# Down matrices of 32 experts: two 2 MB transfers into two ring slots, or one 4 MB transfer into both

## The reference

```python
h = jax.nn.silu(jnp.einsum('td,edf->tef', t, w1)) * jnp.einsum('td,edf->tef', t, w3)
h = h * gate[:, :, None].astype(h.dtype)
y = jnp.einsum('tef,efd->td', h, w2)
```

## Time and profile before

| | us |
|---|---|
| median of 3 runs | 1423.67 (1422.31 to 1424.02) |
| the profiled execution | 1424.06 |
| its span | 1422.3 |
| PE busy | 1359.1 (96%) |
| the chain that ended last, by engine | PE 63%, DMA 18%, DVE 2% |
| DVE, ACT, POOL busy | 539.5, 345.4, 229.4 |
| moved by DMA | 471.66 MB, 332 GB/s over the span |
| the expert transfers | 192 of 2 MB |

### The profile page before, as it was taken

One profiled execution on the slowest core, in us unless ns is written; L12 is line 12 of the kernel. 1 busy time (PEld: TensorE's weight loads), 2 busy tenths in 40 slices (PEclk: granted clock), 3 DMA queues, 4 the chain that ended last, 5 costly groups with the idle time before them and its releaser, 6 DMA issues.

```text
span 1422.3 us, 19177 instructions
## 1 busy us (share of the span) xinstructions
PE 1359.1 (96%) x7242; PEld 766.9 (54%) x7242; DVE 539.5 (38%) x1027; ACT 345.4 (24%) x618; POOL 229.4 (16%) x205
## 2 busy tenths in 40 slices
PE   8999999999999999998998999999999999899896
PEld 7884898987786345434433533544544543443353
DVE  6999420544425233233313323223323231331325
ACT  1121378566571111110210110111111020111102
POOL 2002656687881000000000000000000000000000
PEclk9999999999998999999999999999999999999999
DMA  8533543444475999999999999959999999999992
GB/s 213 178 119 118 207 178 119 156 141 166 139 287 237 388 428 427 429 428 427 429 428 429 429 429 429 428 217 430 429 428 429 428 429 428 429 429 429 428 428 121
DMA packets 71389, 471.66 MB, mean 332 GB/s; under 512 B 17313, under 2 KB 17394, under 8 KB 46130
## 3 DMA queue, kind: packets, MB, share of 16 engines
q1 hardware_dynamic: 70690, 469.75, 80.6%
q10 hardware_dynamic: 528, 1.05, 0.2%
q0 software_dynamic: 128, 0.26, 0.1%
HBM read 468.95 MB, written 2.10 MB: 331 GB/s over the span
## 4 chain that ended last, share of the span: by engine, by line
PE 63%; DMA 18%; DVE 2%; ACT 1%; POOL 1%; issue 1%; DVEq 0%; POOLq 0%; ACTq 0%
PE ps L1870 25%; DMA ring<-in_expert_w_dram 18%; PE ps L1888 12%; PE ps L1528 11%; PE ps L1848 5%; PE ps L1878 3%; PE ps L1899 2%; PE ps L1900 2%; POOL w_lo L558 1%; PE ps L1860 1%; PE ps L1820 1%; PE ps L1795 0%; DVE reg_y L1110 0%; PE ps L1702 0%; DVE reg_x L1463 0%
## 5 line engine op out<-in xcount | busy, mean ns | idle before, releaser
L1888 PE MATMUL ps<-ring,reg_y 128*64 128x512 f32 x1056 | 238.8, 605 | 9.7 <-DVE reg_y L1377 7.8
L558 POOL TENSOR_TENSOR w_lo<-ring,w_hi 128x512 fp32r<-128x512 f32 x152 | 200.0, 1349 | 72.3 <-ACT w_hi L620 71.1
L1383 DVE TENSOR_TENSOR y_lo_t<-ps,y_hi_t 64x512 fp32r<-64x512 f32 x132 | 90.9, 689 | 214.9 <-ACT y_hi_t L852 213.6
L852 ACT ACTIVATE y_hi_t<-ps 64x512 fp32r<-64x512 f32 x132 | 78.1, 592 | 317.9 <-PE ps L1888 315.5
L1888 PEld LDWEIGHTS ps<-ring,reg_y 128*64 128x64 f32 x1056 | 75.4, 139 | 146.7 <-issue 141.5
L1392 DVE TENSOR_TENSOR reg_x<-ps,reg_x 128x512 f32<-128x512 f32 x136 | 87.2, 683 | 137.3 <-PE ps L1900 137.3
L1870 PE MATMUL ps<-reg_e,reg_s 128*64 128x512 f32 x528 | 119.5, 594 | 11.7 <-POOLq L583 11.7
L1870 PE MATMUL ps<-ring,reg_s 128*64 128x512 f32 x528 | 120.0, 596 | 6.8 <-POOLq L583 6.2
L1870 PE MATMUL ps<-ring,reg_y 128*64 128x512 f32 x528 | 120.0, 596 | 6.8 <-POOLq L583 6.2
L1870 PE MATMUL ps<-reg_e,reg_y 128*64 128x512 f32 x528 | 119.5, 594 | 3.2 <-POOLq L583 3.0
L1372 DVE TENSOR_SCALAR reg_y<-ps,lamv 128x512 f32<-128x512 f32 x33 | 24.8, 750 | 244.8 <-PE ps L1870 244.8
(11 more groups left out here) (397 smaller groups left out, 1759.2 us busy)
## 6 DMA issues: line engine op xcount, KB each, us to landing
ring<-in_expert_w_dram SPq DMA_DIRECT2D x128, 2048.0 KB, 20.7
reg_e<-in_expert_w_dram SPq DMA_DIRECT2D x64, 2048.0 KB, 20.9
ring<-in_w_in_dram SPq DMA_DIRECT2D x19, 2048.0 KB, 8.1
ring<-in_w_out_dram SPq DMA_DIRECT2D x8, 2048.0 KB, 8.0
reg_x<-in_x_dram SPq DMA_DIRECT2D x4, 1024.0 KB, 8.5
ring<-in_w_in_dram SPq DMA_DIRECT2D x2, 1024.0 KB, 6.7
out_dram<-reg_x SPq DMA_DIRECT2D x4, 512.0 KB, 2.7
reg_e<-in_ssm_w_glu_dram ACTq DMA_DIRECT2D x1, 1024.0 KB, 9.1
```

Of the source, the lines that this page charges most:

```text
L558: G.tensor_tensor(w_lo[:, i % BUFS, :], unit(u % SLOTS_A)[:, c, :], w_hi[:, i % BUFS, :], ALU.subtract).then_inc(row_lo, 1)
L852: A.activation(y_hi_t[64 * q:64 * q + 64, 512 * k:512 * k + 512], psb[3 + k // 2][64 * (k % 2):64 * (k % 2) + 64, :], cp).then_inc(e_yhi, 1)
L1383: last = V.tensor_tensor(y_lo_t[64 * q:64 * q + 64, w], psb[3 + k // 2][64 * (k % 2):64 * (k % 2) + 64, :], y_hi_t[64 * q:64 * q + 64, w], ...
L1888: last = M(psb[3 + i // 2][64 * (i % 2):64 * (i % 2) + 64, :], hT[:, 2 * half + f, :], unit2(s)[:, f, 512 * i:512 * i + 512], start=half = ...
```

## The change

The down matrix of an expert is now viewed with 4 rows of 8 KB a partition, which are 32 KB in one piece in HBM, and goes in one transfer of 4 MB into ring slots 2 and 3 taken as one tile. Before, each half was a transfer of 16 KB a partition into one slot. SP waits for `slot_free` at the count of piece 5 (both slots free) before it issues this transfer. Its completion raises only the semaphore of ring slot 2, and POOL then raises `e_in` by 2. PE's program is unchanged: `unit2` of slots 2 and 3 finds the same data, since piece 4 was and is the first 16 KB of each partition's 32 KB. The transfers of `w1` and `w3` are unchanged.

```diff
-        w2_v = e_w2.rearrange("l e (p h c) n -> p (l e) h c n", h=2, p=P)
+        w2_v = e_w2.rearrange("l e (p c) n -> p (l e) c n", p=P)
+        w2_slots = ring4[:, 2 * UW:4 * UW].rearrange("p (c n) -> p c n", n=D)
...
             def item(n_, e):
 
-                for k in range(6):
+                for k in range(4):
                     s = slot_of(k)
                     sp.wait_ge(slot_free, n_ * 6 + k + 1)
-                    w = (w1_v, w3_v, w2_v)[k // 2]
-                    src = w[:, ds(e, 1), k % 2, :, :]
-                    sp.dma_start(unit(s) if k < 4 else unit2(s), src.rearrange("p e c n -> p (e c) n")).then_inc(ring_in[s], 16)
+                    src = (w1_v, w3_v)[k // 2][:, ds(e, 1), k % 2, :, :]
+                    sp.dma_start(unit(s), src.rearrange("p e c n -> p (e c) n")).then_inc(ring_in[s], 16)
+                sp.wait_ge(slot_free, n_ * 6 + 6)
+                sp.dma_start(w2_slots, w2_v[:, ds(e, 1), :, :].rearrange("p e c n -> p (e c) n")).then_inc(ring_in[slot_of(4)], 16)
...
             def item_landed(e):
 
-                for k in range(6):
+                for k in range(5):
                     s = slot_of(k)
                     base = 16 * (UNITS_A // SLOTS_A) if s < SLOTS_A else 0
                     g.wait_ge(ring_in[s], e * 16 + base + 16)
-                    g.sem_inc(e_in, 1)
+                    g.sem_inc(e_in, 2 if k == 4 else 1)
```

## The result

The changed kernel takes 1428.89 us in the median of 6 runs (1428.28 to 1431.49), the kernel before 1423.3 us in 6 runs beside it: ratio 1.0044, 95% interval 1.0034 to 1.0054. It is slower by 5.6 us. Run again on another occasion it gave 1429.44 us, ratio 1.005 (1.0032 to 1.0068). The forecast was 1428.9 us; the total was right, but, as the experiments show, two of its four terms had other sizes and one effect was only listed among the rivals, so that the exact hit is partly luck.

What follows compares the result with a forecast made beforehand. PE and DMA were taken to set the pace by turns, by stage. The terms, 3.4 + 0.7 + 3.1 - 2.0 = +5.2 us, gave a median of 1428.9 us, 0.37% slower, range 1424 to 1434.

Steps and rivals of the forecast that it cites:

- term 1: Load 1, short queue: the down matrix is issued at 481.63, not from 478.19, so the stream's gap grows 3.4 us.
- term 2: Restart behind the extra item: load 17's down transfer is issued late, a new gap of 0.7 us, range 0 to 2.
- term 3: PE waits for the whole down matrix: absorbed in the steady stream, 3.1 us at down 31, where nothing absorbs it.
- rival (c): PE's clock falls while idle: 1.7 us more at item 31, 1430.6; at large, past 1435, chance 0.04.
- term 4: Fewer, longer rows in w2 save 0.07 us a load over 28 loads: 2.0 us less, range 0 to 4.5.
- The wait of 2.1 us ahead of down 6: DMA paced stage: down 6 starts 2.1 us later, at its second piece's landing at 640.4; absorbed within two items.
- the groups where DMA leads: Sign: loops of four items where DMA sets the pace repeat every 117 us, shorter by 4 x 0.07.
- none ahead of D's: Sign: PE doesn't idle ahead of the down product of D items, which have the gather ahead of it.
- load 1's down transfer: Sign: SP issues it near 481.6, and the DMA is idle about 4.4 us before it answers.
- what follows down 31: Sign: down 31 starts 3 us behind its turn, and the work after it takes the same time as now.
- the restart behind the extra item: Sign: the DMA pause over the extra item starts and ends 3 us later.
- rival (d): Every transfer pays 1.6 us, queued or not, so one less in 28 loads gives 1386 us; chance 0.01.

Runs made afterwards that it cites:

- the run with the late issue alone: Against the kernel before: SP issues both 2 MB down transfers only when both slots are free, PE starts on the first half; 1427.72 us, ratio 1.0032.
- the run with the one wait: Against the kernel before: PE waits for both down pieces only ahead of item 31's down product; 1428.7 us, ratio 1.0042.

## Why the prediction was right, term by term

| | predicted | measured |
|---|---|---|
| term 1, the gap at load 1 | +3.4 | +2.1 to +2.3 |
| term 2, the restart | +0.7 | +1.2 to +2.6 |
| term 3, the wait for the whole matrix | +3.1 | +3.1 |
| the clock at down 31 | rival (c) | +1.6 to +1.7 |
| term 4, the rate | -2.0 | -2.0 to -2.2 |
| sum | +5.2 | +5.6 and +7.0 (medians) |

**What bounds it** was read rightly: DMA paced stages absorb a delay of PE, PE paced ones a delay of DMA, and each gap is kept where the other side catches up.

**Term 1** had its place right, the size too large. It took the issue times of the down pieces from an execution in which the clock had fallen during item 0's down product. The row was quoted for a rival and not carried to the term beside it. The fall doesn't change the distance between the two issues, 3.44 us with and without it; it puts both 1.7 us later. So the 4 MB were foreseen 26.0 us behind the load's first issue and came at 24.3 (479.14 - 454.80), and the idle time before the answer, foreseen as 4.4 us, was about 2 (321 GB/s over 477 to 484 us). Without the fall the first of two down pieces comes in time and loses nothing, and this slack takes part of the 3.44 us: 1.35 us were lost at w2. The other 0.86, at load 2, had no place in the term. The mean over 16 DMA engines was no great error here, 0.93 us idle for 0.70 + 0.25 in the landings, but it shows idle engines before the piece has landed: the last up piece landed at 481.49, behind that window. Its answer of 1.6 us is also read from the mean; by landings an idle queue takes 2.4 us beyond the bytes. That the profiled pair shows no difference at load 1 is chance: that same fall went with a loss of 2.2 us in the profiled execution of the kernel before (1.3 in the run with rows of 8 KB, which had it too).

**Term 2** was too small. The issue came where it was foreseen: 20.3 us behind the restart, for 967.66 - 947.36. But w2 of load 17 landed 13.3 us after its issue. Its 4 MB take 9.7, which leaves 3.6; the restart's first transfer, into an idle queue, lands 7.3 us after its issue, 2.4 more than its 4.9 (and one of 4 MB, with all three matrices merged, 12.1, again 2.4 more). This one was issued 1.7 us before the piece ahead of it landed, with nothing queued between. Why it comes later than one into an empty queue stays open. It isn't the long rows: the run with the late issue alone, with rows of 16 KB, lost 1.53 us there. Load 19 lost 0 to 2.1 us from one execution to the next, as a transfer that is "just in time" would.

**Term 3** came as worked out. Down 31 was foreseen 9.84 us behind the landing of w3b (1361.3 - 1351.46); it started 9.9 behind it, for 6.8 before, which is 3.1 us. That 1361.13 is so near the 1361.3 of the prediction, which left out its own terms 1, 2 and 4, is luck of this pair: the changed stream was 0.2 us early there, where the terms say 2.1 late. The waits of the steady stream, 3.8 us ahead of down 5 (3.88 measured), are absorbed; the run with the one wait shows that it costs as much as all of them. The wait of 2.1 us ahead of down 6 hardly came (0.27 us), as PE was still late from down 5.

**The clock** was priced at 1.7 us as a rival and left out of the forecast. It fell at down 31 in both profiles of the changed kernel. It fell in the steady stream as well, at each of the five other long waits (down 5, 9, 13, 25 and 29, 8.7 to 10.0 us each), but the down product behind each took 7.09 us again, and PE's 5.8 us to spare covered that, as rival (c) had left open.

**Term 4** was right to the hundredth, 0.07 us a load, though by luck of halving: the line gave 0.13.

The terms that were too small or left out and the one too large cancel, which is luck. Of the signs, the groups where DMA leads (117.17 us), the wait ahead of down 5 and none ahead of D's came; load 1's down transfer was issued at 479.14, not near 481.6, what follows down 31 is later by the clock's 1.6 us too, and the restart behind the extra item came 1.64 us earlier, not 3 us later, since the kernel before had lost as much at load 1 in this pair.

The rule on transfer size from the Trainium skill (SBUF — State Buffer, The DMA setup-cost knee), weighed as rival (d), doesn't hold for queued transfers here: the merging of two into one left the group at 117.49 us for 117.47. The Trainium skill's ceiling of 435.2 GB/s (DMA: Bandwidth & Descriptors, Where 436 GB/s comes from) isn't passed: 4 MB in 9.71 us are 432 GB/s.

## What to carry to other kernels

In a ring that streams weights, the size of a transfer is also the size of a slot: a larger one is issued later, lands as a whole later, and keeps fewer in the queue, and this is paid where the queue is short (start, restart behind an overload, tail), not where it is full. Before pricing a gap, list the landings of single transfers rather than mean shares of the DMA engines, and check whether the execution at hand carries an accident, such as a fallen clock, in the rows used. A wait that a bound stage hides in the loop is paid once, in full, at the last item, and an idle TensorE there may pay again with its clock; four products on idle data held the clock up here, in the one profile taken, without a gain in time that the runs resolve.

## What the runs showed of the hardware

With rows of 8, 16 and 32 KB in a third of the bytes, 48 MB take 118.06, 117.47 and 117.17 us, which is 9 to 10 ns a row and DMA engine beyond its bytes. The number of transfers costs nothing while the queue is fed (117.49 us with one of 4 MB, 117.47 with two of 2 MB). Behind the extra item, a transfer of 2 MB into the idle queue lands 7.3 us after its issue, one of 4 MB 12.1 us, each 2.4 beyond its bytes; in the changed kernel, one of 4 MB issued 1.7 us before the only piece ahead of it lands took 12.6 to 13.3 us, 2.9 to 3.6 beyond its bytes. The clock can fall at the same instruction in some executions and not in others: item 0's down product took 8.78 us in two profiles (the kernel before and the run with rows of 8 KB) and 7.09 in the other nine, and down 31, behind its ordinary wait of 0.98 us, 7.09 us in three profiles and 8.80 in a fourth. Behind a wait of about 4 us with no work in it, down 31 took 8.7 to 9.9 us in all six profiles.
